# Layer 1's mixing, done per token block between the gather slots of the block ahead

## The reference, cut to what matters

```python
for i in range(DEPTH):                      # DEPTH = 2
    h = _rmsnorm(x, norm_mix[i])
    f = h @ w_in[i] + b_in[i]               # 1024 -> 768 attention + 1824 rwkv columns
    attn = _rmsnorm(_swa_sink_attention(q, k, v, sinks), attn_out_norm[i])  # chunks of 64, own and previous chunk
    rw = _rwkv7_mix(f[..., OFF_RWKV:], ...) # token shift, decay, delta-rule state carried over all tokens
    x = x + concat([attn, rw]) @ w_out[i]
    x = x + _peer(_rmsnorm(x, norm_ffn[i]), peer_wq[i], peer_keys[i], peer_u[i], peer_v[i])
    gate = sigmoid(_rmsnorm(x, norm_ple[i]) @ ple_gate[i])
    x = x + (p[i] @ ple_proj[i]) * gate
return _rmsnorm(x, norm_final)
```

## Time and profile before

| what | us |
|---|---|
| time, median of 3 runs (lowest to highest) | 1790.77 (1790.53 to 1791.15) |
| the profiled execution's own time | 1791.59 |
| its span, first to last instruction | 1789.5 |
| first gather issued | 206.7 |
| first and last dot of layer 0 | 213.2 and 865.1 |
| first and last dot of layer 1 | 1103.4 and 1756.7 |

### The profile page before, as it was taken

One profiled execution on the slowest core, in us unless ns is written; L12 is line 12 of the kernel. 1 busy time (PEld: TensorE's weight loads), 2 busy tenths in 40 slices (PEclk: granted clock), 3 DMA queues, 4 the chain that ended last, 5 costly groups with the idle time before them and its releaser, 6 DMA issues.

```text
span 1789.5 us, 24016 instructions
## 1 busy us (share of the span) xinstructions
PE 1501.2 (84%) x8581; PEld 847.2 (47%) x8581; DVE 1244.1 (70%) x2903; ACT 790.3 (44%) x2289; POOL 658.0 (37%) x556
## 2 busy tenths in 40 slices
PE   8999488888987987788899994888889789787876
PEld 7988444444432433333489873444444334332323
DVE  5776677777777787776467766777776777777754
ACT  5563344444444444333366433444443444444343
POOL 0010244444444455544000102445445454554540
PEclk9999799999999989999999997999999999999999
DMA  7312499999999999999452124999999999999992
GB/s 297 119 49 87 176 427 425 426 427 423 427 426 427 392 414 427 427 426 427 189 189 96 49 107 199 427 427 426 426 427 415 427 427 397 424 426 427 426 427 102
DMA packets 83774, 604.49 MB, mean 338 GB/s; under 512 B 9296, under 2 KB 9424, under 8 KB 10704
## 3 DMA queue, kind: packets, MB, share of 16 engines
q0 software_dynamic: 73728, 536.90, 71.6%
q1 hardware_dynamic: 9936, 66.21, 9.7%
HBM read 602.03 MB, written 1.05 MB: 337 GB/s over the span
## 4 chain that ended last, share of the span: by engine, by line
PE 47%; DMA 26%; DVE 16%; ACT 6%; issue 3%; POOL 1%; SPq 0%; ACTq 0%; POOLq 0%; DVEq 0%
DMA gath<-in_experts,idx 25%; PE PS L1550 24%; PE PS L1206 9%; DVE gath L1099 6%; PE PS L1222 2%; ACT diag L641 2%; PE PS L1575 2%; PE PS L1411 1%; PE PS L1438 1%; PE PS L1594 1%; POOL gath L380 1%; DMA praw<-in_p_t 1%; DVE topi L1051 1%; PE PS L1463 1%; DVE topi L1044 1%
## 5 line engine op out<-in xcount | busy, mean ns | idle before, releaser
L1550 PE MATMUL PS<-gath,diag 128*128 128x512 f32 x2048 | 980.9, 623 | 250.9 <-ACT diag L641 250.3
L380 POOL DMA_INDIRECT gath<-in_experts,idx x512 | 625.7, 1222 | 709.9 <-PE PS L1550 547.2
L1099 DVE CUSTOM_DVE_ANT_0 gath<-gath,xn 128x1024 f32<-128x1024 f32 x512 | 618.2, 1222 | 322.9 <-DMA gath<-in_experts,idx 321.8
L1550 PEld LDWEIGHTS PS<-gath,diag 128*128 128x128 f32 x2048 | 380.5, 196 | 810.5 <-ACT diag L641 452.6
L629 ACT ACTIVATE stat<-hid 128x1 f32<-128x1 f32 x512 | 103.4, 202 | 598.6 <-DVE hid L1099 598.1
L641 ACT ACTIVATE diag<-cst,stat 128x128 f32<-128x128 f32 x512 | 205.6, 402 | 48.3 <-ACT stat L637 1.1
L729 DVE TENSOR_TENSOR low<-ring,high 128x1024 fp32r<-128x1024 f32 x110 | 133.5, 1222 | 86.5 <-ACT high L403 86.3
L1206 PE MATMUL PS<-hTh,high 128*128 128x256 f32 x592 | 179.5, 303 | 4.8 <-DVE hTl L750 3.1
L1206 PE MATMUL PS<-hTl,high 128*128 128x256 f32 x592 | 167.1, 282 | 0.0
L1206 PE MATMUL PS<-hTh,low 128*128 128x256 f32 x592 | 166.9, 282 | 0.0
L637 ACT ACTIVATE stat<-stat,gate 128x1 f32<-128x1 f32 x512 | 143.3, 280 | 0.1
(11 more groups left out here) (271 smaller groups left out, 1459.6 us busy)
## 6 DMA issues: line engine op xcount, KB each, us to landing
ring<-in_w_slabs SPq DMA_DIRECT2D x58, 1024.0 KB, 5.3
gath<-in_experts,idx POOLq DMA_INDIRECT x512, 10.7
xres<-in_x SPq DMA_DIRECT2D x2, 512.0 KB, 4.7
gffn<-in_gain_ffn SPq DMA_DIRECT2D x2, 512.0 KB, 5.8
out<-xn SPq DMA_DIRECT2D x2, 512.0 KB, 5.2
cst<-in_consts SPq DMA_DIRECT2D x1, 680.0 KB, 10.7
praw<-in_p_t SPq DMA_DIRECT2D x1, 512.0 KB, 15.4
gfin<-in_g_final SPq DMA_DIRECT2D x1, 512.0 KB, 7.6
```

The source lines that it names most:

```text
L380: pool.indirect_dma_start(gath[:, n % NB], None, experts[L], bass.IndirectOffsetOnAxis(ap=idx[:, tb, h, k:k + 1], axis=0)).then_inc(landed ...
L1099: dve.tensor_tensor_reduce(out=u, in0=u, in1=xn[:, i // SLOTS], scale=1.0, scalar=0.0, op0=ALU.mult, op1=ALU.add, accum_out=hid[:, i:i + 1 ...
L1550: ins = mm(PS[:, 2 * tb + s], diag[:, n % ND], gath[:, n % NB, D + 512 * s:D + 512 * (s + 1)], start=i % SLOTS == 0, stop=i % SLOTS == SLO ...
```

## The change

Layer 0 keeps its mixing and its order. The loop over layers is gone. The expert slots are now four units `u` of 128 (layer 0 block 0 and 1, layer 1 block 0 and 1), each engine going through them with a function `upto(u, t)` that does all slots up to slot `t` of unit `u`. Between them stand `tail(u)`, the end of the layer for the block of unit `u`, and `mix(b)`, layer 1's mixing of block `b` alone, both placed in unit `u + 1` (for `mix(b)`, `b = u`) at slots that a table gives:

```diff
-NB, ND = 8, 4
-RANKINGS = TB * PH
+NB, ND = 7, 4
+UNITS = DEPTH * TB
...
+IN_ORDER = (0, 1, 2, 3, 4, 5, 18, 19, 20, 10, 11, 12, 13, 6, 7, 8, 9, 14, 15, 16, 17)
+SLAB_ORDER = (0, 1, 2, 9, 10, 5, 6, 3, 4, 7, 8)
...
+AT = dict(
+    summed=2, rows_tr=3, squared=4, rows=5, gate=7, sigmoid=16, proj=17, gated=18,
+    square=20, xn=22, tr=23, hT=24, inp=25, evac=26,
+    mix_lora=36, mix_k=40, mix_r=44, mix_v=48,
+    vt=32, vt_out=33, sc0=33, lg0=35, sc1=35, lg1=37, exps=38, pt0=39, pt0_out=41, pt1=41, pt1_out=43, pv=43, ao=45, ao_sq=46, ao_ms=47,
+    ao_n=49, aoT=49, aoT_out=51,
+    lora_in=37, a_up=37, a_out=39, w_up=39, w_out=41, g_up=41, g_out=42, csum=43, decay=44,
+    kss=42, kmax=44, rn=45, kmod=45, kkn=47, bonus=48, bonus_v=50, arbt=49,
+    tok0=48, tok0_out=50, tok1=50, tok1_out=51, prod0=51, tok2=52, tok2_out=53, mask0=53, prod1=54, mask1=55, xinit=55, xinit_out=57,
+    level=57, period=3, chunk0=73, chunk1=79, yT=87, ym=89, out0=84, out1=89, added=94,
+    square2=95, xn2=97, tr2=97, hT2=99, hn=101, q=100, q_out=102, s=102, s_out=104, keys=105, pairs=106, experts=107, exp0=107, gates=109)
```

```diff
+    for u in range(1, BLOCKS):
+        base, L, b = SLOTS * u, (u - 1) // TB, u - 1
+        if u >= TB:
+            items += [(base + TOPK * h + 0.5, 1, S_WQ + 1 + h, u) for h in range(PH - 1)]
+        items += [(base + AT["gate"] + 2 * j, L, S_PLE + 1 + j, u - 1) for j in range(4)]
+        items += [(base + AT["proj"], L, S_PLE, u - 1)]
+        if u <= TB:
+            first = 0
+            for n in SLAB_ORDER:
+                items += [(base + AT["inp"] + first, 1, n, b)]
+                first += 1 if n == S_LORA - 1 else 2
+            items += [(base + AT["a_up"] - 1.5, 1, S_LORA, b)]
+            items += [(base + (AT["out0"], AT["out0"] + 2, AT["out1"], AT["out1"] + 2)[j], 1, S_OUT + j, b) for j in range(4)]
+            items += [(base + AT["q"], 1, S_WQ, TB + b)]
+    items += [(SLOTS * BLOCKS - 28, 1, S_PLE, BLOCKS - 1)]
+    items += [(SLOTS * BLOCKS + j, 1, S_PLE + 1 + j, BLOCKS - 1) for j in range(4)]
```

PE's input tile, a level and the slot loop of the changed kernel:

```diff
+                    w = slab(1, m // 2, b)
+                    for k in range(KT):
+                        ins = mm(PS[:, 4 + p % 2, 0:P], w[:, m % 2 * D + k * P:m % 2 * D + (k + 1) * P], hB[:, k], start=k == 0, stop=k == KT - 1)
+                    ins.then_inc(part_used, 1)
...
+                for lv in range(LEVELS - 1):
+                    at("level", AT["period"] * lv)
+                    pe.wait_ge(x_made, 20 + (LEVELS - 1) * b + lv + 1)
+                    mm(PS[:, 4, 0:CHUNK], nil, nil[:, 0:CHUNK], start=True, stop=True)
+                    for s, c in group:
+                        ins = mm(PS[half(1 - c), A[s // 4], columns(s)], MoneB[half(c), s], XB[half(c), s], start=True, stop=True)
...
+                    at("level", AT["period"] * lv + 2)
+                    pe.wait_ge(px_ready, 20 + (LEVELS - 1) * b + lv + 1)
+                    pe.wait_ge(xs_made, 20 + (LEVELS - 1) * b + lv + 1)
...
+                while done[0] < SLOTS * u + min(t, SLOTS):
+                    n = done[0]
+                    v, h, j = n // SLOTS, n % SLOTS // TOPK, n % TOPK
+                    pe.wait_ge(diag_made, n + 1)
+                    for s in range(2):
+                        ins = mm(PS[:, 2 * (v % TB) + s], diag[:, n % ND], gath[:, n % NB, D + 512 * s:D + 512 * (s + 1)],
+                                 start=n % SLOTS == 0, stop=n % SLOTS == SLOTS - 1, skip_group_check=True)
+                    ins.then_inc(spent, 1)
```

More of the change, by code:

```diff
@@ L73, in half, with streamed @@
+STREAM = stream()
+PLACE = {item[1:]: q for q, item in enumerate(STREAM)}
+def streamed(layer, slab, whose):
+    q = PLACE[layer, slab, whose]
+    return q % RING, 16 * (S_PLE // RING + q // RING + 1)
 def half(c):
@@ L305, in wait_free @@
                     return
[L306 to L321, removed]
@@ L716, in _ @@
+            scores_out(3)
+            exponentials(0, 0)
+            upto(0, SLOTS)
+            for u in range(BLOCKS):
+                at = lambda name, more=0, u=u: upto(u + 1, AT[name] + more) if u + 1 < BLOCKS else None
+                tail(u, at)
+                if u < TB:
+                    mix(u, at)
+                if u + 1 < BLOCKS:
+                    upto(u + 1, SLOTS)
         @block.vector
@@ L731, in norm @@
             def norm(r, gain, meanwhile=None):
[L732 removed]
+                for tb in range(TB):
                     normalized(r, tb)
@@ new lines, in _ @@
+            product(0)
+            product(1)
+            for g in range(2):
+                sets = slice(8 * g, 8 * g + 8)
+                dve.wait_ge(prod_ready, 4 * L + 2 * g + 2)
+                dve.tensor_tensor(Mone[:, sets], prods[:, sets, 0], eye, ALU.add).then_inc(dve_step, 1)
+                steps[0] += 1
+                if g == 0:
+                    product(2)
+                dve.wait_ge(dve_step, steps[0])
+                dve.tensor_tensor(XT[:, sets], Mone[:, sets], first_mask, ALU.mult).then_inc(xm_ready, 2)
+                if g == 0:
+                    product(3)
@@ new lines, in _ @@
+            experts_found(0, 0)
+            for m in range(4, 8):
+                split(projection_tile(0, "wq", m))
+            gates_made(0, 0)
+            dve.wait_ge(hn_ready, 1)
+            upto(0, SLOTS)
+            for u in range(BLOCKS):
+                at = lambda name, more=0, u=u: upto(u + 1, AT[name] + more) if u + 1 < BLOCKS else None
+                tail(u, at)
+                if u < TB:
+                    mix(u, at)
+                elif u == TB:
+                    at("xn")
+                    written(0)
+                else:
@@ new lines, in _, with slab, block_queries @@
+            done = [0]
+            def slab(layer, n, whose):
+                slot, count = streamed(layer, n, whose)
+                pe.wait_ge(filled[slot], count)
+                return ring[:, slot]
+            def block_queries(u, h):
+                w, b, v = slab(1, S_WQ + h, u), u - TB, PH * (u - TB) + h
+                if v:
+                    pe.wait_ge(psc_ready, 16 + v)
+                for c in range(2):
+                    for k in range(KT):
+                        ins = mm(PS[:, 7, c * P:(c + 1) * P], w[:, c * D + k * P:c * D + (k + 1) * P], hQ[:, k], start=k == 0, stop=k == KT - 1, skip_group_check=True)
+                ins.then_inc(uq_ps, 1)
```

2495 lines of the change are left out of this document (1528 added, 967 removed).

## The result

| kernel | median us | lowest to highest | runs |
|---|---|---|---|
| before | 1790.73 | 1787.74 to 1794.17 | 18 |
| after | 1796.49 | 1788.13 to 1801.88 | 18 |

The ratio is 1.0028 (95% 1.0016 to 1.0040): the change makes the kernel slower by 0.3%, where the prediction had 1739 us and a range up to 1795. The profiled execution of after took 1793.8 us, its span is 1792.0.

A forecast was written before the change was run, and what follows sets the result against it. The prediction saw two bounds in turn: DMA engines in the units, the PE-DVE-ACT chain in the gap. DMA alone 1696.3 + 22 (stretches) + 4 (ACT) + 15 (waits) = 1737.3 us span, 1739 us with 1.3 around it; range 1700 to 1795.

The forecast's parts named there:

- the sooner spend of the last slot: End of unit 4: the multiplier follows its own gelu, 2.4 us from dot to spend for 4.6, ending about 1.5 us sooner.
- the tail: After the last dot: 32.8 us before, plus 4 us for the plain gate products, less 1.5; 35 us expected.
- NB = 7: Gather buffers: seven for eight cost nothing, since the shorter buffer life hides the loss.
- The two slots of slack: Gather buffers: fastest landing 6.8 us, median 10.7, so some two slots (5 us) of slack stay.
- each stretch goes at its slowest engine: Units 2 and 3: buffers even out only 5 us; excess over DMA 12 + 10 = 22 us.
- 15 for waits: Hand-overs between engines, some 45 a block: 15 us in all, from a possible 0 to 135 us for 90.
- PE's work: Units 2 and 3: PE has 332 of 374 and 364 of 392 us, with spends 220 a unit; fits on average.
- Slots 43 to 57: Keys, decay, token order, products: DVE 47 us against DMA 37 (unit 3: 40), excess 10 and 7 us.
- Slots 72 to 128: Last stretch of units 2 and 3: DMA ahead, no excess; POOL's four pow steps a block cost nothing.
- The ACT tables: Slots 37 to 43: ACT 33 us against 30, at 1.28 us a table load; 2 us a block, 4 in all.
- Rival 3: Slower: PE waits at each of 90 in-order hand-overs; at 1.2 us each 1832 us; chance 0.11.
- Rival 2: Units 2 and 3 run at a chain, ACT's blocks and DVE late behind them: 40 us more, about 1779; chance 0.22.

The follow-up runs named there:

- the small slabs: The changed kernel with each slab streamed in the units loading only its first 128 of 2048 columns: 1757.61 us, ratio 0.9827.
- the tables: The changed kernel with every exp, sigmoid and tanh of the per-block mixing on ACT made an identity, no table loads: 1779.16 us, ratio 0.9917.
- another: The changed kernel with the ranking of the next layer's head 0 moved from slots 105 to 109 to slots 112 to 118: 1781.98 us, ratio 0.9947.
- Input tiles, tables and both moves together: The changed kernel with group norm and head 0 ranking steps later, 6 of 8 in-projection products a tile and mixing table loads left out: 1749.75 us.
- the lightest kernel: The changed kernel, mixing steps spread later, without mixing table loads and most in-projection, output, level and layer 1 query products: 1727.27 us, ratio 0.9654.
- the first move: The changed kernel with the second half of the group norm (DVE's use of the inverse roots) six slots later: 1774.01 us, ratio 0.9902.

## Why the prediction was wrong

**Right.** The gap of 235.8 us went and nothing took its place on the path. Slabs, traffic (640 MB), unit 4, the sooner spend of the last slot and the tail came within 5 us each; PE is busy over 90% in slots 57 to 72 (40.0 of 41.0 and 45.4 of 48.6 us). NB = 7 with the direct multiplier costs nothing (1788.9 us).

**Wrong in its reason: "Without it a lost slot of slack costs where engines stall, not in steady flow."** The sum held because two effects of 36 us cancel. The two slots of slack, inferred from landings of 6.8 to 10.7 us, did not exist; one slot less costs 36 us over steady units. With seven buffers and the old order the fastest landing is 5.3 and the median 9.6 us, for 6.8 and 10.7: with fewer gathers in flight a landing got shorter, so its length did not say how many are needed.

**The step that failed: in units 2 and 3 "each stretch goes at its slowest engine", plus 4 us for ACT and 15 for waits.** It gave 41 us above the transfers, measured are 93. It failed in three terms.

*PE's work.* The prediction had "332 of 374 us" in unit 2 and "364 of 392" in unit 3, and "On average PE fits"; busy are 361 and 391. In unit 3 that is as long as the transfers. The difference is in the spends, 250 us a unit for 220; all the rest is 112 and 141 us for 112 and 144. The price of 0.43 us a record, taken from one full stretch, holds where PE is full, as in unit 2 of after:

```profile
642.18 1.88 PE L2022 MATMUL PS<-gath,diag 128*128 128x512 f32 x4
643.90 1.95 PE L2092 MATMUL PS<-hB,ring 128*128 128x128 f32 x16
645.68 1.88 PE L2022 MATMUL PS<-gath,diag 128*128 128x512 f32 x4
```

From start to start the spend takes 1.72 us and the tile 1.78, as priced. But a spend behind which PE stands counts 1.98 us (rows of the tail), and one at the lower clock up to 3.4. The trace of before had this already: its 2048 records are busy for 980.9 us, 245 a unit, not 220. So a part of the 30 us is only how a stand is counted. Of the lower clock an estimate can be given: a mean of 0.97 over 414.7 us is worth at most 12 us of work. "PE at 2.4 GHz throughout" is false.

*Slots 43 to 57*, priced by DVE's 47 us of work: 58.4 and 64.4, the largest single miss (29 of the 71 us by which the stretches exceed their forecasts, against which the forecast had 19 without a place). PE is busy 50.0 and 55.8 us there, where the prediction had 41 to 47, and stands for 8.4 and 8.6. DVE is not full (38.8 and 38.4 us); it waits 14.2 and 16.3 us for `kmax`, and just before, in slots 36 to 43 of unit 2, 11.1 for the sigmoid that the scan of the decays reads. The prediction saw that work lies two slots apart and took PE's spends in between as cover; DVE is ahead by the buffers and first has to wait until PE is there. What the wait for `kmax` alone costs is not shown: PE stands 2.5 us behind it in the rows above, and no run moves that step alone.

*Slots 72 to 128*, costed at nothing: 10 and 14 us. "POOL gets four pow steps a block between its gathers", with "so nothing" at its end, looked at POOL's load and its own wait for keys, not at who waits behind a gather for the `pow`: 7.5 us in unit 2 and 6.6 in unit 3 by the run that moved it. The ranking of the next layer's head 0 in the same slot as the regular one was not looked at.

**The ACT tables.** 4 us forecast, 12 to 17 measured. One load is still 1.28 us; twenty fewer are 25.7 us of ACT, of which half to two thirds were on the path. At the 2.7 us that the Trainium skill (ScalarE: Activation LUTs, "Rules for kernel authors") budgets for a switch, twenty would have been 54 us, an estimate. The trace does not agree: in ACT's timeline a load starts at 904.15 and the next instruction at 905.44, 1.29 us for the switch. The page's advice to do all of one table set before switching was not tried here.

**The rivals.** Rival 3 had the sign, but not the form: PE does not wait at each of 90 hand-overs, it stands for more than 1 us at about ten places a block, 28 us in unit 2 between slots 25 and 112. Rival 2 names some of them (ACT's blocks, DVE late behind them). Its sign, "PE idle behind ACT in units 2 and 3 over 30 us", is met (48.7 us in unit 2 alone), but says little: the kernel before has 250 us of the same wait in all, wherever its units wait for gathers. What fits the runs best is that three limits lie close together. 56 us of PE's work gave 39 when taken away, the small slabs 39 (20 of them in units 2 and 3), the tables 17, one move 22, another 14. Input tiles, tables and both moves together gave 47 where the single ones add up to over 78, and the last 7 and 20 us of the lightest kernel stay unexplained. That PE's work counts is shown by runs, and that the first move takes away the stand at slot 79. That the lower clock behind each stand is what made this move worth 22 us is only argued; over whole units its share hardly differs from the kernel before (0.97 for 0.95 to 0.97), and it also comes in slots that no edit touches.

The change is worth having with one step moved: 1774.0 us, 1% below the kernel before, by four executions.

## What to carry to other kernels

When work is placed between the steps of a pipeline, count the distance of two steps in the reader's time: an engine that may run seven buffers ahead of the other comes to its step up to seven slots early, and a result of the slower engine has to be asked for that much later, or its lead is spent in waiting. The one move of this kind, six slots for a result of POOL behind PE, gave 22 us by the medians and 13.5 by the profiled spans. Follow a wait through every queue, also through an engine that is hardly used, and ask what stands in front of the awaited instruction. A price taken from a full stretch is a lower bound; where two engines' sums are within 10% of each other, as here, expect more than the larger of the two.

## What the hardware showed that I had not expected

- One gather buffer of eight, with the same life, is worth 2% (1827.25 us for 1791.5); with a life shorter by about 2 us it is worth nothing (1787.94 against 1788.9).
- The granted clock falls to its lower level behind stands of 3.4, 2.7, 2.5 and 5.0 us (not behind those of 1.9 and 2.1 us before 900.1 and 904.2), and a 16-record tile that meets it takes 3.1 to 3.6 us for 1.95.
- The share of the DMA engines can be near 1 while they move less than their best. A window of after, slots 67 to 72 of unit 2, and one of the kernel with the first move, slots 84 to 92:

```profile
783.00:795.70 12.70, 12.70 (x152) 7.02 (x151) 9.90 (x24) 5.59 (x18) 4.99 (x5) 1.00 0.99 358
...
824.00:850.20 26.20, 26.20 (x91) 11.78 (x91) 20.55 (x53) 10.37 (x29) 9.38 (x9) 1.00 1.01 427
```

Where the earlier trace rows have 426 GB/s at 1.01, the first has 358 at 0.99, as the earlier trace rows had 357 at 0.98. The second has 427, with PE as full: that PE is busy does not by itself slow the transfers, as the prediction read the earlier trace rows. In the kernel with the least of PE's work eleven of the fifteen stretches of unit 2 are at 417 GB/s or more. The kernel before with seven buffers shows a share of 1.00 at 411 GB/s, with no more of PE's work, so the share stays near 1 also when fewer gathers are in flight. Whether the packets themselves are slowed, or the share counts time in which a queue has little to send, no run here tells apart.
